# A two-layer hybrid decoder step on one core: six exchanges of order in the in-projection stage

## The reference, cut to what matters

```python
h = x @ w_in                                   # 20 column tiles of 128
u_a, q_b, k_b, v_b, q_c, k_c, v_c, g_c = split(h)
# S5 branch: diagonal complex state space, then a gated unit
y = s5_scan(u_a) @ C + d * u_a
hh = gelu(y)
ya = rms_norm(hh * sigmoid(hh @ w_glu))
# stick-breaking attention (prompt: causal; samples: paged cache)
z = q_b @ k_b.T / 8 + bias
log_rest = -softplus(z)                        # = log_sigmoid(z) - z, where valid
tail = reverse_cumsum(log_rest) - log_rest
yb = rms_norm(exp(log_sigmoid(z) + tail) @ v_b)
# retention
inner = (rope(q_c) @ rope(k_c).T) * decay
o = inner @ v_c (+ state for the samples)
yc = silu(g_c) * group_norm(o)
x = layer_norm(ALPHA * x + concat(ya, yb, yc) @ w_out)
x = layer_norm(ALPHA * x + conv_ffn(x))
```

## Time and profile before

| what | value |
|---|---|
| time, median of 3 runs | 669.62 us (668.28 to 669.98) |
| the profiled execution, its own time | 669.83 us |
| its span, first to last instruction | 668.0 us |
| busy PE / DVE / ACT / POOL | 98% / 82% / 64% / 19% |
| mean granted TensorE clock | 0.997 |
| PE idle in the span | 14.4 us |

### The profile page before, as it was taken

One profiled execution on the slowest core, in us unless ns is written; L12 is line 12 of the kernel. 1 busy time (PEld: TensorE's weight loads), 2 busy tenths in 40 slices (PEclk: granted clock), 3 DMA queues, 4 the chain that ended last, 5 costly groups with the idle time before them and its releaser, 6 DMA issues.

```text
span 668.0 us, 14231 instructions
## 1 busy us (share of the span) xinstructions
PE 653.6 (98%) x5400; PEld 620.4 (93%) x5400; DVE 549.4 (82%) x1169; ACT 425.6 (64%) x718; POOL 124.4 (19%) x160
## 2 busy tenths in 40 slices
PE   9999979999999999999999999999999999999997
PEld 7878958999999999999987998989999999999996
DVE  6899967989998988789768897698999898874753
ACT  5788447758666666643848854776766676663343
POOL 0054020050222222200037010106022222120011
PEclk9999989999999999999999999999999999999999
DMA  8776521646674665473537574464766556656511
GB/s 317 243 292 215 174 97 64 242 123 226 216 249 153 199 187 185 148 259 128 189 124 255 177 213 144 131 220 138 208 211 200 180 185 194 177 185 195 160 56 67
DMA packets 43207, 122.33 MB, mean 183 GB/s; under 512 B 5570, under 2 KB 15202, under 8 KB 42626
## 3 DMA queue, kind: packets, MB, share of 16 engines
q1 hardware_dynamic: 40754, 115.68, 53.1%
q0 software_dynamic: 1088, 4.11, 2.5%
q10 hardware_dynamic: 1296, 1.63, 0.7%
HBM read 115.79 MB, written 5.61 MB: 182 GB/s over the span
## 4 chain that ended last, share of the span: by engine, by line
PE 88%; DVE 6%; ACT 3%; issue 1%; DMA 1%; DVEq 0%; ACTq 0%
PE ps L490 21%; PE ps L491 20%; PE ps L492 20%; PE ps L483 6%; PE ps L554 4%; PE ps L502 2%; PE ps L503 2%; PE ps L504 2%; DVE ring_lo L1725 1%; DVE z L1622 1%; PE ps L670 1%; DVE z L1630 1%; PE ps L891 1%; ACT L1092 1%; PE ps L824 1%
## 5 line engine op out<-in xcount | busy, mean ns | idle before, releaser
L1718 DVE TENSOR_TENSOR w_lo<-ring,w_hi 128x1024 fp32r<-128x1024 f32 x144 | 175.4, 1220 | 31.1 <-ACT w_hi L1071 29.2
L490 PE MATMUL ps<-x_hi,w_hi 128*128 128x264 f32 x672 | 191.1, 284 | 1.0 <-DVE x_lo L1668 1.0
L491 PE MATMUL ps<-x_lo,w_hi 128*128 128x264 f32 x672 | 190.5, 283 | 0.0
L492 PE MATMUL ps<-x_hi,w_lo 128*128 128x264 f32 x672 | 190.4, 283 | 0.0
L1071 ACT CAST w_hi<-ring 128x1024 fp32r<-128x1024 f32 x144 | 150.1, 1043 | 61.1 <-PE ps L492 56.4
L490 PEld LDWEIGHTS ps<-x_hi,w_hi 128*128 128x128 f32 x672 | 126.6, 188 | 1.8 <-issue 1.8
L491 PEld LDWEIGHTS ps<-x_lo,w_hi 128*128 128x128 f32 x672 | 126.7, 189 | 0.0
L492 PEld LDWEIGHTS ps<-x_hi,w_lo 128*128 128x128 f32 x672 | 126.0, 188 | 0.0
L490 PE MATMUL ps<-hff_hi,w_hi 128*128 128x264 f32 x352 | 100.2, 285 | 0.0
L492 PE MATMUL ps<-hff_hi,w_lo 128*128 128x264 f32 x352 | 100.0, 284 | 0.0
L491 PE MATMUL ps<-hff_lo,w_hi 128*128 128x264 f32 x352 | 99.8, 283 | 0.0
(11 more groups left out here) (410 smaller groups left out, 1314.6 us busy)
## 6 DMA issues: line engine op xcount, KB each, us to landing
ring<-in_units SPq DMA_DIRECT2D x187, 512.0 KB, 3.6
kv<-in_kpool SPq DMA_DIRECT2D x32, 128.0 KB, 2.5
kv<-in_vpool SPq DMA_DIRECT2D x32, 128.0 KB, 2.9
SR<-in_sret SPq DMA_DIRECT2D x2, 1024.0 KB, 6.5
out_rsample<-SR POOLq DMA_DIRECT2D x2, 1024.0 KB, 5.3
out_kv<-hb ACTq DMA_DIRECT2D x2, 528.0 KB, 5.3
VBC<-v_rows POOLq DMA_DIRECT2D x8, 128.0 KB, 3.3
out_y<-x SPq DMA_DIRECT2D x3, 264.0 KB, 2.1
```

Of the source, the lines that this page charges most:

```text
L490: mm(out, wh, hi, start=start, stop=False)
L491: mm(out, wh, lo, start=False, stop=False)
L492: return mm(out, wl, hi, start=False, stop=stop)
L1718: E.did(tt(w_lo[:, slot], ring[:, ring_slot(L * UNITS + i)], w_hi[:, slot].bitcast(F32), ALU.subtract), "w_lo")
```

## The change

Six places, none of which adds or removes arithmetic.

1. PE, layer 0, tile 16: the order was `v_samples`, `ret_inner`, `k_transposes`, `s5_glu`, `transposes`; it becomes `s5_glu`, `ret_inner`, `k_transposes`, `v_samples`, `transposes`.
2. ACT, layer 0, tile 16: `v_spread` stood ahead of the sigmoid; it comes behind it, ahead of `v_tokens`.
3. ACT, layer 0, tile 10: the high half of unit 13 is made ahead of the decay of the retention state (`SR`, L1400), no longer behind it.
4. ACT, layer 0, tile 17: the order was `square_a`, the high half of unit 22, `open_gates`, `square_b`; it becomes `open_gates`, `square_a`, `square_b`, the high half of unit 22.
5. DVE, layer 0: `sb_second` moves from behind `s5_scan(1)`, the low half of unit 13 and `s5_skip(0)` to ahead of all three. The low half of unit 13 also moves ahead of the scan.
6. DVE, layer 1: `sb_second` moves from behind `s5_scan(1)` and `s5_skip(0)` to ahead of both.

```diff
-EARLY_MOVED = [(9, 14, 16), (4, 5)]
+EARLY_MOVED = [(9, 10, 14, 16), (4, 5)]
@@ PE
-                    if L == 0 and i == at_["vb"]:
-                        v_samples(L)
                     if i == at_["c1"]:
                         s5_c(L, 1)
                     if i == at_["tails"]:
                         sb_tails(L)
-                    if L > 0 and i == at_["glu"]:
+                    if i == at_["glu"]:
                         s5_glu(L)
                     if i == at_["inner"]:
                         ret_inner(L)
                     if i == at_["kt"]:
                         k_transposes(L)
-                    if L == 0 and i == at_["glu"]:
-                        s5_glu(L)
+                    if L == 0 and i == at_["vb"]:
+                        v_samples(L)
                     if L == 0 and i == at_["vt"]:
                         transposes(L)
@@ ACT
-                    if L == 0 and i == at_["vb"]:
-                        v_spread(L)
+                    if L == 0 and i == 10:
+                        split_hi_early(L, i + EARLY_BY)
                     if i == at_["srg"]:
...
                         E.did(f(sg[:], ps[:, 2:4, 0:T], ACT.Sigmoid), "sig")
                     if L == 0 and i == at_["vt"]:
+                        v_spread(L)
                         v_tokens(L)
                         split_hi_early(L, i + EARLY_BY)
...
                     if L == 0 and i == at_["out"]:
+                        open_gates(L)
                         square_a(L)
+                        square_b(L)
                         split_hi(L, N_IN + 2)
-                    if i == 17:
+                    if L > 0 and i == 17:
                         open_gates(L)
-                        if L == 0:
-                            square_b(L)
@@ DVE, layer 0
                     split_lo_early(L, 12)
+                    sb_second(L)
+                    split_lo_early(L, 13)
                     s5_scan(L, 1)
-                    split_lo_early(L, 13)
                     s5_skip(L, 0)
-                    sb_second(L)
                     split_lo_early(L, 14)
```

## The result

The changed kernel takes 664.55 us in the median of four runs (663.72 to 665.62), the one before 669.64 us beside it (668.28 to 669.98). The ratio is 0.9929, with a 95% interval of 0.9905 to 0.9952: 5.1 us or 0.7% less. The profiled execution took 665.36 us for a span of 663.5 us.

What follows compares the result with a forecast made beforehand. The prediction took PE, busy 653.6 of 668.0 us, to bound the kernel, with its waits and the low clock behind the longest. Gains of 4.2 + 0.8 + 0.7 = 5.7 us from 669.62 gave 663.9 us, range 662.5 to 666.4.

Steps and rivals of the forecast that it cites:

- case A: Layer 0, tile 16: the clock stays up behind the remaining 1.9 us gap; 663.9 us (662.8 to 664.9), chance 0.60.
- B: Layer 0, tile 16: the remaining 1.9 us gap still lowers the clock; 665.5 us, chance 0.22.
- the prediction's own sign of being wrong: Wrong if value rows wait over 2.5 us, 1.2 GHz follows them, or PE waits anew between tile 17 and out projection.
- What bounds the kernel: PE, busy 653.6 of 668.0 us; layer 0's gap at tile 16 costs 5.2 us, 1.7 of it low clock.
- Softplus and unit 13, layer 0: Softplus finds its input ready by 0.15 us, and PE's whole 1.0 us wait ahead of tile 13 goes.
- The lead of DVE: Layer 0: DVE is 0.4 us ahead (0.3 to 0.6) when it reaches the rotation.
- Tile 16: Layer 0: value rows wait 1.9 us for RI instead of 3.02 and 0.47; tile 17 starts 4.2 us earlier.
- rival E: Layer 0: value rows reach VBC so late that DVE's states and PE wait; 672.1 us at 12 us more, chance 0.03.
- Gates: Layer 0: PE's 0.60 us wait ahead of the second mean of squares goes; 0.8 us gained.
- Layer 1: The tails start 1.4 us earlier, 0.7 us comes back as tile 12's wait for its low half; 0.7 us remains.
- Rival C: The mean's 0.8 us and layer 1's 0.7 us are taken back; gain near 4, 665.7 us, chance 0.11.
- The sum: Whole kernel: 4.2 us at tile 16, 0.8 for the squares and 0.7 in layer 1 make 5.7 us less.

Runs made afterwards that it cites:

- filled kernel before: The kernel before with seven float32 products without a use put into PE's 3.02 us gap at tile 16 of layer 0; 668.48 us against 669.9.
- filled changed kernel: The changed kernel with four products without a use put into PE's 1.79 us gap ahead of the value rows of layer 0; 663.77 us.
- e1_tile16: Only places 1 and 2 of the change, made on the kernel before; 666.79 us against 669.82.
- e3_softplus0: Only places 3 and 5 of the change, made on the kernel before; 669.2 us, ratio 0.9995.
- f3_no_softplus0: The changed kernel with the page products moved ahead of the value rows, into the gap, but without places 3 and 5; 663.01 us against 662.28 with them.
- e2_gates: Only place 4 of the change, made on the kernel before; 668.93 us, ratio 0.9986.
- e4_softplus1: Only place 6 of the change, made on the kernel before; 669.91 us, ratio 1.0005.

## Why the prediction was right, point by point

The forecast was 663.9 us, 662.5 to 666.4; the median is 664.55 us. It came out so because cases A and B of the prediction, 663.9 and 665.5, both happened: two runs at 663.73 and two at 665.5. Either would have been inside the range; that the median is within 0.7 us of the forecast owes something to the two runs with the clock up. By the prediction's own sign of being wrong, a stretch at 1.2 GHz behind the value rows, case A failed in the two others, the profiled one among them.

- **What bounds the kernel.** PE's waits, and the clock behind the longest. The filled kernel before measures the clock's price directly: 1.68 us, where I had 1.7.
- **Softplus and unit 13, layer 0.** As stated: softplus not late, no wait ahead of tile 13. The lead of DVE was mis-sized: RI starts 31.91 us after the first S5 output product (87.37 - 55.46) against 32.66 before (87.72 - 55.06), so 0.75 us and not 0.4, outside my bounds of 0.3 to 0.6. The part up to the low half 14 is 0.44, and the second skip gave 0.35, where I had put 0.1 for it.
- **Tile 16.** The wait that takes the place of the old one was named (value rows for RI) and sized 1.9 us; it is 1.79. With the clock up (the filled changed kernel), X falls from 48.08 to 43.56, 4.5 us, where I had 4.2 for the part to tile 17; with it low, 2.9 us. The 4.5 us are 1.80 us of waiting from places 1 and 2, 1.04 us from places 3 and 5, and 1.68 us of low clock. (The prediction's own figures, 100.12 less 95.8, make 4.3 and not 4.2, and RI ends in it at 89.4 where the next sum takes 89.5.) POOL's issues stand at 93.58 (predicted 94) and DVE reaches the states at 105.03 with no wait, so rival E was far off.
- **Clock.** Here the weights failed. I gave B 0.22, since 1.9 us lies nearer to 1.38 than to 3.02. In two of the changed kernel's four runs and three of ten of e1_tile16, both with a gap of 1.8 us, the clock fell all the same: 5 of 14, so a chance nearer to a third would have fitted better.
- **Gates.** 0.8 us forecast, 0.64 to 0.86 measured. The table loads have no drain behind them: the sigmoid begins 0.10 us after its table (84.49 + 1.28 = 85.77, 85.87). The section "What ACT_TABLE_LOAD costs" of the Trainium skill (*ScalarE: Activation LUTs*) gives 1.38 us for that drain; the trace does not agree.
- **Layer 1.** 0.7 us forecast, 0.53 measured. The wait of tile 12 is 0.90 us and not 0.7; PE is there a little earlier than I had it. Rival C, that such wins are taken back, holds for 0.9 of the 1.4 us here, of which the sum had 0.7, and for nothing of the gates up to the state product. The 0.53 us rests on the traces alone; no times show it.
- **The sum.** 4.2 + 0.8 + 0.7 against 4.5 + 0.85 + 0.53 with the clock up: 5.7 and 5.9 us.

In the expectations of the experiments the gap of e1_tile16 (1.3 for 1.78 us) and the DVE lead in e3_softplus0 failed, as told there. And where the expectation of f3_no_softplus0 says that in the changed kernel the 1.0 us ahead of tile 13 came back as a longer gap, the 1.04 us from e1_tile16 to the filled changed kernel say that it did not. What stays open is what decides, from run to run, whether the clock falls behind one and the same gap.

## What to carry to other kernels

When an exchange ends one wait of the bounding engine, write down who frees the next resource in line: here the bank that DVE frees last was claimed first, and putting the value rows, which claim it, back to the front, or a piece that needs nothing of DVE into the gap, was worth another 2.3 us at the median. A wait ahead of a longer wait is worth what its end brings the engine that ends the longer one, and that is to be read from that engine's own timeline: the 1.0 us ahead of tile 13 gave 0.82 us ahead of the 3 us gap, 1.04 us ahead of the 1.8 us gap and 1.03 us without a gap. The times showed this only among runs of one clock, so judge small moves on a version without the gap, or sort the runs by clock. And price a gap with the clock behind it, measured by filling it with idle products.

## What was not expected of the hardware

- A gap of 1.8 us on TensorE lowered the clock in some runs and not in others of one kernel: 2 of 4 and 3 of 10 runs had a mean granted clock of 0.996 to 0.997. Behind the 3.0 us gap of the kernel before it was 38 of the 55 runs taken beside the experiments, at 0.993 to 0.997 (median 670.0 us, and 668.2 us for the other 17). The length of the gap alone does not decide: the profiled run of e3_softplus0 kept a granted clock of 1.00 behind 3.23 us, where the changed kernel's fell behind 1.79. With the gap filled or gone (46 runs) none was under 0.998.
- It cost 1.6 to 1.7 us in both kernels in which it was measured, with the glu products behind the gap in one and transposes and page products in the other. The 32 small page products stretched too, from 1.91 to 2.74 us.
- The kernel before (9 runs), e2_gates (1), e3_softplus0 (4) and e4_softplus1 (1) also had runs at 0.993 to 0.995. Those of the first three are 0.7 to 1.5 us above the median of the same kernel's runs at 0.996 and 0.997, that of e4_softplus1 only 0.4 us. None of them was profiled, so what they lost it to stays open.
